# Expert items of 128 rows with an fp32 tail of up to 32 rows, in place of items of one or two 128-row blocks

## The reference

```python
logits = (xt @ w_router + b_router)
top_val, top_idx = lax.top_k(logits, TOP_K)      # 4 of 32 experts for each of 1024 tokens
gates = jax.nn.softmax(top_val, axis=-1)
...
gu = rows @ w_gate_up[e] + b_gate_up[e]          # 1024 -> 2048
gate = jnp.minimum(gu[:, :D_FF], SWIGLU_LIMIT)
up = jnp.clip(gu[:, D_FF:], -SWIGLU_LIMIT, SWIGLU_LIMIT)
hid = (up + 1.0) * (gate * jax.nn.sigmoid(gate * SWIGLU_ALPHA))
return hid @ w_down[e] + b_down[e]               # 1024 -> 1024
```

## Time and profile before

| | |
|---|---|
| median of 3 executions | 2768.33 us (2766.95 to 2768.82) |
| the profiled execution | 2765.02 us |
| its span in the profile | 2763.4 us |
| granted TensorE clock, mean | 0.965 of full speed |
| busy: PE, DVE, ACT | 92%, 62%, 48% |
| expert stage, first bias row on PE to last store of `ysb` | 844.4 to 2547.3 us of the span |

### The profile page before, as it was taken

One profiled execution on the slowest core, in us unless ns is written; L12 is line 12 of the kernel. 1 busy time (PEld: TensorE's weight loads), 2 busy tenths in 40 slices (PEclk: granted clock), 3 DMA queues, 4 the chain that ended last, 5 costly groups with the idle time before them and its releaser, 6 DMA issues.

```text
span 2763.4 us, 37051 instructions
## 1 busy us (share of the span) xinstructions
PE 2537.6 (92%) x11003; PEld 1855.1 (67%) x11004; DVE 1701.2 (62%) x2447; ACT 1318.7 (48%) x1535; POOL 201.5 (7%) x188
## 2 busy tenths in 40 slices
PE   6999999868848999999999999999999999998687
PEld 3456666544426778787777878787878888777233
DVE  4653333523355796779779696768676657774354
ACT  2113333332223774658577484657564445562232
POOL 1100000001220000000000000000000000000210
PEclk9999999988868999999999999999999999999799
DMA  5009500322215896879789696869685666783541
GB/s 177 19 12 339 186 20 22 109 81 69 68 42 187 301 355 215 293 242 369 240 302 354 217 348 237 290 226 341 218 286 199 203 207 231 246 286 129 192 144 49
DMA packets 387538, 556.36 MB, mean 201 GB/s; under 512 B 18241, under 2 KB 326977, under 8 KB 387362
## 3 DMA queue, kind: packets, MB, share of 16 engines
q1 hardware_dynamic: 333922, 456.55, 49.4%
q10 hardware_dynamic: 39408, 57.67, 5.7%
q0 software_dynamic: 14160, 41.51, 4.4%
HBM read 482.91 MB, written 71.19 MB: 201 GB/s over the span
## 4 chain that ended last, share of the span: by engine, by line
PE 63%; issue 6%; DVE 6%; ACT 1%; DMA 1%; DVEq 1%; SPq 0%; ACTq 0%; POOLq 0%; POOL 0%
PE bank L554 16%; PE bank L552 16%; PE bank L553 16%; PE bank L1274 5%; PE bank L647 4%; PE bank L546 2%; PE bank L523 1%; DVE wlo L711 1%; PE bank L531 1%; PE bank L650 1%; DVE sig L732 1%; PE bank L1286 1%; DVE xlo L716 1%; DVE gat L727 0%; DVE upc L728 0%
## 5 line engine op out<-in xcount | busy, mean ns | idle before, releaser
L1458 ACT ACTIVATE whi<-raw 128x2048 fp32r<-128x2048 f32 x384 | 733.4, 1917 | 578.5 <-PE bank L554 532.2
L711 DVE TENSOR_TENSOR wlo<-raw,whi 128x2048 fp32r<-128x2048 f32 x384 | 876.2, 2286 | 210.4 <-PE bank L554 195.6
L552 PE MATMUL bank<-whi,xhi 128*128 128x512 f32 x1472 | 577.1, 392 | 0.0
L554 PE MATMUL bank<-wlo,xhi 128*128 128x512 f32 x1472 | 574.3, 390 | 0.0
L553 PE MATMUL bank<-whi,xlo 128*128 128x512 f32 x1472 | 573.8, 390 | 0.0
L554 PEld LDWEIGHTS bank<-wlo,xhi 128*128 128x128 f32 x1472 | 276.5, 188 | 58.1
L553 PEld LDWEIGHTS bank<-whi,xlo 128*128 128x128 f32 x1472 | 276.8, 188 | 57.1
L552 PEld LDWEIGHTS bank<-whi,xhi 128*128 128x128 f32 x1472 | 276.9, 188 | 54.1
L552 PE MATMUL bank<-whi,hhi 128*128 128x512 f32 x736 | 292.1, 397 | 0.0
L554 PE MATMUL bank<-wlo,hhi 128*128 128x512 f32 x736 | 287.3, 390 | 0.0
L553 PE MATMUL bank<-whi,hlo 128*128 128x512 f32 x736 | 287.0, 390 | 0.0
(11 more groups left out here) (263 smaller groups left out, 2853.6 us busy)
## 6 DMA issues: line engine op xcount, KB each, us to landing
raw<-in_w_gate_up_dram SPq DMA_DIRECT2D x512, 512.0 KB, 4.7
raw<-in_w_down_dram SPq DMA_DIRECT2D x128, 1024.0 KB, 6.9
expert_rows<-zeros ACTq DMA_DIRECT2D x1, 32768.0 KB, 103.8
expert_rows<-ysb ACTq DMA_DIRECT2D x46, 512.0 KB, 6.2
xall<-in_x_dram SPq DMA_DIRECT2D x8, 512.0 KB, 10.2
uT<-in_w_out_dram SPq DMA_DIRECT2D x1, 4096.0 KB, 14.2
xr<-in_x_dram SPq DMA_DIRECT2D x8, 512.0 KB, 6.4
h_scratch<-h SPq DMA_DIRECT2D x8, 512.0 KB, 2.8
```

Source lines behind the costliest of these rows:

```text
L552: pe.matmul(dst, stat_hi[:, b, kt], hi, start=False, stop=False)
L554: return pe.matmul(dst, stat_hi[:, b, kt], lo, start=False, stop=last)
L711: dve.tensor_tensor(wlo[:, c % LO], raw[:, c % RAW], whi[:, c % HI].bitcast(F32), ALU.subtract).then_inc(lo_ready, 1)
L1458: act.activation(whi[:, c % HI], raw[:, c % RAW], ACT.Copy).then_inc(hi_ready, 1)
```

## The change

- The item table: an item is one expert with up to 128 rows. Rows 129 to 160 of an expert are a *tail* of its item (the field `TWO` now means "has a tail"). An expert with more than 160 rows gets a further item, which loads and splits all its weights again. There are no two-block items. With the counts above this makes 38 items, of which 8 have a tail: 32 experts, and a second item for 6 of them.
- A tail's rows are multiplied in plain fp32 with the raw pieces in `raw`, not with whi and wlo. `tail_piece` puts four products with 32 stationary columns on four column groups of the array. For gate/up each group takes one of the four 128-deep parts of the piece, and `tail_sum` adds the four groups with one product by a 0/1 matrix. For down each group makes 256 of the 1024 columns. ACT, DVE and PE do sigmoid, clamp, product and transposes for the tail with their own small buffers (`tail_sigmoid`, `tail_gated`, `turn_tail_hidden`, `tail_hidden`).
- SP may overwrite a slot only when PE's tail product has read it too (`tail_free`, in `slot_free`).
- POOL fetches the tail's rows and the expert's biases, spread to 32 partitions.
- The transposes of the next item's rows are cut into two halves, after pieces 7 and 9.
- The second group of the item loop now runs: 6 of its 32 passes have an item, 26 have none.

The core of the difference:

```diff
-BLK = 2 * P
-MAX_ITEMS = E + T * TOPK // (BLK + 1)
+TAIL = 32
+GROUPS = P // TAIL
+MAX_ITEMS = E + T * TOPK // (P + TAIL + 1)
...
+                                    body(n, k1, True)
                                     eng.reg_add(self.twos, self.twos, 1)
                                 with eng.Else():
-                                    body(n, k1, (0,))
-
-        def gate_bank(blocks, b, q):
-            return banks(2 * b + q % 2) if len(blocks) == 2 else banks(2 + q % 2)
-
-        def down_bank(b, d):
-            return banks(2 * b + d)
+                                    body(n, k1, False)
...
+            def turn_tail_rows(n, k1):
+                pe.wait_ge(xgt_in, 16 * k1 + 16)
+                hold(pe, xlo_ready, 2 * n + 2)
+                for k in range(KD):
+                    mm = pe.transpose(banks(XT)[:, k * TAIL:k * TAIL + TAIL], xgt[0:TAIL, k * P:k * P + P],
+                                      ident[0:TAIL, 0:TAIL])
+                mm.then_inc(xtt_done, 1)
...
+            def tail_piece(k1, c):
+                if c == 0:
+                    pe.wait_ge(xt_ready, k1 + 1)
+                    pe.wait_ge(ytail_ready, k1)
+                if c in (2, 4, 6, 8):
+                    pe.wait_ge(sums_ready, 4 * k1 + c // 2)
+                if c >= 8:
+                    pe.wait_ge(ht_ready, 4 * k1 + c - 7)
+                if c < 8:
+                    half = c % 2
+                    for j in range(GROUPS):
+                        mm = pe.matmul(banks(ACC)[j * TAIL:j * TAIL + TAIL, :], xt[:, half * 4 + j], raw[:, c % RAW, j],
+                                       start=(half == 0), stop=(half == 1))
+                else:
+                    r = c - 8
+                    for kk in range(2):
+                        for j in range(GROUPS):
+                            mm = pe.matmul(banks(ACC)[j * TAIL:j * TAIL + TAIL, 0:256], htail[:, 2 * r + kk],
+                                           raw[:, c % RAW, 2 * kk + j // 2, j % 2 * 256:j % 2 * 256 + 256],
+                                           start=(r == 0 and kk == 0), stop=(r == 3 and kk == 1))
+                mm.then_inc(tail_free, 1)
+            def tail_sum(k1, j):
+                pe.wait_ge(sums_ready, 4 * k1 + j + 1)
+                pe.wait_ge(ht_ready, 4 * k1 + j)
+                pe.matmul(banks(SUM)[0:TAIL, :], sel[:], sums[:], start=True, stop=True).then_inc(u_done, 1)
+            def turn_tail_hidden(k1, j):
+                hold(pe, hid_t_ready, 4 * k1 + j + 1)
+                for h in range(2):
+                    mm = pe.transpose(banks(SUM)[:, h * TAIL:h * TAIL + TAIL], hid_t[0:TAIL, h * P:h * P + P],
+                                      ident[0:TAIL, 0:TAIL])
+                mm.then_inc(htt_done, 1)
...
+                    mm = gate_piece(n, c) if c < 8 else down_piece(n, c)
+                    mm.then_inc(w_free, 1)
+                    if c in (3, 5, 7):
+                        turn_hidden(n, (c - 3) // 2)
+                    if tail:
+                        if c in (2, 4, 6, 8):
+                            tail_sum(k1, c // 2 - 1)
+                        if c in (3, 5, 7, 9):
+                            turn_tail_hidden(k1, (c - 3) // 2)
+                        tail_piece(k1, c)
                     if c == 4:
                         items.ahead(n + 1)
                         nxt, nxt2 = items.value(LIVE), items.value(TWO)
+                    if c in (7, 9):
+                        with pe.If(nxt > 0):
+                            turn_rows(n + 1, (c - 7) // 2)
+                    if c == 11:
                         with pe.If(nxt2 > 0):
+                            turn_tail_rows(n + 1, nk1)
...
+            def tail_sums(k1, j):
+                if j == 0:
+                    dve.wait_ge(bias_t_in, 80 * k1 + 80)
+                dve.wait_ge(u_done, 4 * k1 + j)
+                dve.wait_ge(tail_free, PIECES * k1 + 2 * j + 2)
+                dve.tensor_tensor(sums[:].rearrange("p (h n) -> p h n", h=2),
+                                  banks(ACC).rearrange("p (h n) -> p h n", h=2),
+                                  bias_t[:].rearrange("p (h q n) -> p h q n", h=2, q=4)[:, :, j, :],
+                                  ALU.add).then_inc(sums_ready, 1)
+            def tail_clamp(k1, j):
+                src = banks(SUM)[0:TAIL]
+                dve.wait_ge(u_done, 4 * k1 + j + 1)
+                dve.wait_ge(hid_t_ready, 4 * k1 + j)
+                dve.tensor_scalar(gat_t[0:TAIL], src[:, 0:256], LIMIT, None, ALU.min).then_inc(gat_t_ready, 1)
+                dve.tensor_scalar(upc_t[0:TAIL], src[:, 256:512], LIMIT, -LIMIT, ALU.min, ALU.max).then_inc(upc_t_ready, 1)
+            def tail_gated(k1, j):
+                dve.wait_ge(sig_t_done, 4 * k1 + j + 1)
+                dve.tensor_tensor(sig_t[0:TAIL], gat_t[0:TAIL], sig_t[0:TAIL], ALU.mult).then_inc(gs_t_done, 1)
+                dve.wait_ge(gs_t_done, 4 * k1 + j + 1)
+                dve.wait_ge(htt_done, 4 * k1 + j)
+                dve.scalar_tensor_tensor(out=hid_t[0:TAIL], in0=upc_t[0:TAIL], scalar=1.0, in1=sig_t[0:TAIL],
+                                         op0=ALU.add, op1=ALU.mult).then_inc(hid_t_ready, 1)
+            def tail_rows(k1):
+                dve.wait_ge(tail_free, PIECES * k1 + PIECES)
+                dve.wait_ge(ytail_out, 64 * k1)
+                dve.tensor_tensor(ysb_t[:], banks(ACC)[:, 0:256], bias_d[:], ALU.add).then_inc(ytail_ready, 1)
...
+                    if tail and c in (3, 5, 7, 9):
+                        tail_gated(k1, (c - 3) // 2)
                     if c in (1, 3, 5, 7):
+                        dve.wait_ge(w_free, PIECES * n + c + 1)
+                        clamp(n, (c - 1) // 2)
+                        if tail:
+                            tail_sums(k1, (c - 1) // 2)
...
+                            two, tails = read(sp, n, TWO), read(sp, n, NTWO)
+                            def slot_free(c):
+                                read_by_tail = sp.snap(tails * PIECES + two * (c + 1), min_val=0, max_val=MAX_ITEMS * PIECES)
+                                hold(sp, lo_ready, PIECES * n + c + 1)
+                                sp.wait_ge(tail_free, read_by_tail)
                             for c in range(RAW, PIECES):
-
-                                sp.wait_ge(lo_ready, PIECES * n + c - RAW + 1)
+                                slot_free(c - RAW)
                                 expert_piece(sp, e, c, c % RAW)
                                 if c == RAW:
                                     sp.reg_mov(live_r, read(sp, n + 1, LIVE))
@@ -986,14 +1082,17 @@
                                 sp.reg_mov(expert_r, read(sp, n + 1, EXPERT))
                                 e2 = sp.snap(expert_r, min_val=0, max_val=E - 1)
                                 for c in range(RAW):
-                                    sp.wait_ge(lo_ready, PIECES * n + RAW + c + 1)
+                                    slot_free(RAW + c)
...
+                    k = read(pool, n, NTWO)
+                    e = read(pool, n, EXPERT)
+                    hold(pool, xtt_done, k)
+                    pool.dma_start(ids_t[0:TAIL], list_dram[bass.ds(row + P, TAIL), :]).then_inc(ids_t_in, 16)
+                    hold(pool, ids_t_in, 16 * k + 16)
+                    pool.indirect_dma_start(out=xgt[0:TAIL], out_offset=None, in_=u2_dram,
+                                            in_offset=bass.IndirectOffsetOnAxis(ap=ids_t[0:TAIL], axis=0)
+                                            ).then_inc(xgt_in, 16)
+                    hold(pool, ytail_ready, k)
+                    pool.dma_start(bias_t[0:TAIL], b_gate_up[0, bass.ds(e, 1), :].rearrange("e n -> (e n)")
+                                   .partition_broadcast(TAIL)).then_inc(bias_t_in, 16)
...
+            def tail_sigmoid(k1, j):
+                act.wait_ge(gat_t_ready, 4 * k1 + j + 1)
+                act.activation(sig_t[0:TAIL], gat_t[0:TAIL], ACT.Sigmoid, scale=ALPHA).then_inc(sig_t_done, 1)
+            def tail_hidden(k1, j):
+                act.wait_ge(htt_done, 4 * k1 + j + 1)
+                act.activation(htail[:, 2 * j:2 * j + 2].rearrange("p k n -> p (k n)"), banks(SUM)[:, 0:2 * TAIL],
+                               ACT.Copy).then_inc(ht_ready, 1)
...
+            def tail_rows_out(k1, row):
+                act.wait_ge(ytail_ready, k1 + 1)
+                for j in range(GROUPS):
+                    act.dma_start(y_dram[bass.ds(row + P, TAIL), j * 256:j * 256 + 256],
+                                  ysb_t[j * TAIL:j * TAIL + TAIL]).then_inc(ytail_out, 16)
...
+                        sigmoid(n, (c - 1) // 2)
+                    if tail and c in (2, 4, 6, 8):
+                        tail_sigmoid(k1, c // 2 - 1)
                     if c in (3, 5, 7):
+                        hidden(n, (c - 3) // 2)
+                    if tail and c in (3, 5, 7, 9):
+                        tail_hidden(k1, (c - 3) // 2)
...
```

(9 more changed lines are left out.)

425 lines of the change are left out of this document (208 added, 217 removed).

## The result

| | before | changed |
|---|---|---|
| median of the runs | 2768.32 us | 3103.24 us (3101.77 to 3105.25, 4 runs) |
| ratio to before | | 1.1216, 95% interval 1.1200 to 1.1233 |
| profiled execution, its span | 2765.02, 2763.4 | 3103.04, 3101.4 |
| mean granted clock | 0.965 | 0.915 |
| expert stage, first bias row to last store | 1702.9 | 842.6 to 2866.7, 2024.1 |

The change makes the kernel 12% slower. The prediction was 3000 us, slower, with a range of 2895 to 3120. The sign and the range hold; the number is 103 us low.

A forecast was written before the change was run, and what follows sets the result against it. It took the expert stage to be bound by PE, busy 92% of the span. 2765.0 + 211 (expert stage) + 17 (empty passes) + 4 (start) = 2997, with 3.3 for the median 3000 us, range 2895 to 3120.

The forecast's parts named there:

- The ring: Items with a tail: slot release, load, ACT's split and next tail product wait in turn; eight whole loads, 72.4 us.
- rival 1: The ring does not bind and an item with a tail is DVE-bound at about 50 us: 2640 us in all; chance 5%.
- Eight links: Steps 2 to 9 and 9 to 11 of an item with a tail, each holding a whole load; sum 72.4 us.
- T: An item with a tail: 97 us, against 70.4 for the two-block item it replaces.
- Pieces 0 to 2 before the ring: Start of an item with a tail: 3 x 3 us and a sum, 10.1 us.
- The last T: The last item with a tail loads no next item, so links 6 to 9 run at PE's pace: 80 us.
- S after a T: One-block item after a tail item: raw slots empty, late splits, 1.5 us for each of 6, 9 in all.
- S: A one-block item without a tail: unchanged except for halved transposes, 38.1 us each, 30 of them 1143 us.
- A rival with the right number and the wrong cause: Runs of one-block items are held by DMA, 39 us or more each: 3030 us in all; chance 8%.
- Column groups: A tail piece's four products on four column groups overlap: 0.85 us a piece, bounds 0.43 and, with no overlap, 3.4.
- Changes of the tile's shape: 24 changes of shape on PE in an item with a tail, left unpriced; at 0.15 us each, 29 us more in all.
- Empties: At the expert stage's end each engine passes 26 empty items at 0.65 us: +17 us, bounds 8 and 74.

The follow-up runs named there:

- the order mended: Against the second form: in one-block items too ACT's split stands last in its step, ACT's and DVE's next-item columns come first in steps 8 and 10; 2695.2 us.
- the second form: Changed kernel with GROUP 19, DVE's columns first in step 9, and in tail items each ACT split a whole step later; 2753.2 us, ratio 0.9949.
- The shorter load: Changed kernel with half of piece 11 not loaded, so half of that piece's products use old weights; 3090.7 us, ratio 1.118.

## Why the prediction was right, and where it was 103 us short

**The ring (its rival 1, refuted) was right, in mechanism and in size.** Eight links were priced at 72.4, with tail pieces and clock at 84.4. In the tail item from 1187.3 SP issues the load that tail piece 2 releases (down piece 8), and the one that tail piece 11 releases (the first half of the next item's gate piece 5), at these times:

```profile
1203.28 32.03 SPq L484 DMA_DIRECT2D raw<-in_w_down_dram  x4
...
1288.24 0.37 SPq L477 DMA_DIRECT2D raw<-in_w_gate_up_dram  x1
```

That is 85.0 us. The two runs that cut into the ring, at ACT or at SP, took most of T's excess away. Inside it one term was not priced, ACT's table load of 1.28 us ahead of the first sigmoid. ScalarE: Activation LUTs ("What ACT_TABLE_LOAD costs") of the Trainium skill has the same 1283 ns, but adds a drain that makes it 2.66 us; here the load starts as the split ends, and the sigmoid starts 0.02 us after the load, so this case does not show the drain. One sign was named too low: PE was to be half busy in the ring.

```profile
1187.30:1192.00 4.70, 4.15 (x17) 3.25 (x16) 1.82 (x1) 2.18 (x2) 0.00 (x0) 0.69 0.75 223
...
1204.00:1288.00 84.00, 53.53 (x243) 30.95 (x241) 35.31 (x47) 22.45 (x27) 2.32 (x2) 0.82 0.33 110
```

It is busy 53.5 us of the 84.0, or 64%, at a mean granted clock of 0.82.

**T: 97 predicted, 105.7 measured.** The two ends of the ring were mis-sized.
- "Pieces 0 to 2 before the ring take 3 x 3 us and a sum", 12.7 with their tail pieces. It took 16.0, from 1187.3 to 1203.3. The prediction took the full clock there; in the first 4.7 us the mean granted clock is 0.69 (the first line above). That this is all of the 3.3 us is not shown.
- The prediction let T end with the ring. But after tail piece 11 has released its slot it is 4.7 us to the store, because ACT copies the rows only after it has split a piece whose load was issued at 1284.3.

Seven T together: +61. The last T was predicted at 80 and took 77.6.

**S after a T: +1.5 predicted, about +7 measured**, 33 us over six. The step "the raw slots are empty and the next S starts with late splits" saw the late pieces but not who stands behind them. ACT in the S that starts at 1292.9, in order of time:

```profile
1298.93 1.28 ACT L1572 ACT_TABLE_LOAD   x1 [1.52 <-PE bank L586]
1300.32 1.91 ACT L1572 ACTIVATE whi<-raw 128x2048 fp32r<-128x2048 f32 x1
1303.59 1.91 ACT L1572 ACTIVATE whi<-raw 128x2048 fp32r<-128x2048 f32 x1 [1.36 <-DMA raw<-in_w_gate_up_dram]
1305.52 1.28 ACT L1586 ACT_TABLE_LOAD   x1
1306.81 0.42 ACT L1586 ACTIVATE sig<-gat 128x256 f32<-128x256 f32 x1
```

DVE had the gate ready at 1297.5. ACT takes its sigmoid at 1306.8, behind the splits of pieces 6 and 7, of which the second waits for its load, and behind two table loads. DVE idles 7.2 us for it and PE 7.0 us for DVE. It is the same order that makes the ring. Late loads and the order both have a part: with the loads out of the ring and ACT's order as it was such an S took 42.0, and with the order mended 4.4 less than in the second form.

**S: 38.1 predicted, 38.98 measured**, 22 us over 24. "An S stays as it is: its transposes are halved, nothing else" is the failed step. The second half of transposes needs the bank that the first half leaves, so a chain PE, ACT, DVE, PE now runs inside pieces 8 and 9, and PE waits 1.2 us at its end. PE's wait ahead of these transposes in the S from 955.1 of the kernel before, and its other wait in the S from 1337.7 now:

```profile
PE bank L523 <- issue: 0.2, 1, 0.2
```
```profile
PE bank L573 <- DVE hlo L803: 0.6, 1, 0.6
```

All of PE's named waits come to 1.0 us in the first of these items and to 1.8 in the second, which is nearly all of the loss of 0.9 us. That it is order and not PE's work or the loads is shown: with the halves kept and ACT's splits last in their steps, S takes 36.5 us early in a row and PE waits 0.4 of them. A rival with the right number and the wrong cause stood close by: 39 us by DMA. The shorter load refuted it.

**Column groups:** four at once, and 0.85 us for a piece at the full clock was right, but by luck. The prediction took a record for a product. Each product is two records, 0.43 us apart at the full clock and 0.86 at half. The 16 records of the full-width line of the earlier trace rows are the eight products of one sum over k in the source, so a full-width fp32 product takes 0.86 us too (7.03 / 8 is 0.88), and the lower bound of 0.43 could not be reached. The eight records on 64 rows are four products, two at a time, and their stretch (570.8 to 574.2) has a granted clock of 0.61, not 1.00. So an fp32 product costs the same on a part of the array as on all of it; what column groups give is four of them in the time of one. The prediction set the Trainium skill's four passes for true FP32 (FP8 and Floating Point Precision, "TensorE Precision Notes") against the full width; by the estimate of 0.85 us made from them there, the trace agrees at full width too.

**Changes of the tile's shape:** set aside in the prediction, at 29 us if each cost 0.15. Runs show that they do cost something. A down piece of the last T, at the full clock:

```profile
2861.50 0.39 PE L586 MATMUL bank<-wlo,hhi 128*128 128x512 f32 x1
2861.82 1.07 PE L639 MATMUL bank<-raw,htail 128*32 128x256 f32 x16
2862.82 0.50 PE L584 MATMUL bank<-whi,hhi 128*128 128x512 f32 x1
2863.16 0.40 PE L585 MATMUL bank<-whi,hlo 128*128 128x512 f32 x1
```

Products of one shape follow each other here at 0.23 us, and the 16 records of 256 columns, four at a time, need 4 x 0.215. From the first line to the last that would be 1.32 us, and it is 1.66. So a tail piece costs about 0.3 us more than its products, 4 us in a T of 12 pieces and some 30 in eight, as an estimate. Where a load sets the pace this is partly hidden; where PE does, it is part of T's 56 to 58 us.

**Empties: 17 predicted.** Last store to the end grew by 18.6 us, and the chain shows a pass each 0.66 us. Right, and branches are not dear: no empty pass took longer. The Trainium skill's rule on a taken branch (Runtime: NRT & Kernel Launch, "Instruction fetch mechanics") is for a target outside the pages of instructions that an engine holds; no stall of that kind shows, and no run tells whether these jumps leave those pages.

**Start: +4 predicted, -1.8 measured.** Neither can be told: in the other profiled executions, whose start is the same but for a step or two of the table, the first bias row comes at 841.1 to 845.6 us.

The sum: T +61 - 2.4 - 3 (for biases, not seen), S after T +33, S +22, that is +110 in the stage; end +1.6; start -5.8: 106 over the predicted span of 2995. The profiled execution is this time at the median and not 3.3 below it, and 103 are left.

## What to carry to other kernels

When a buffer gets a second and later reader, follow its release through every engine's queue: if the release waits for something that stands behind the next load's consumer, each step costs a whole load, however idle the engines are. On an engine that both takes in loads and serves a short chain, put the chain's work ahead of the wait for a load, and give the load a step of slack; here this, with the same order for the next item's columns and 0.4% from fewer empty passes, turned 12% slower into 2.6% faster. Then read the item after the odd one too: it starts with what the odd one left unloaded.

## What was not expected of the hardware

- Four fp32 products with 32 stationary columns each, on four column groups and into one bank, take as long as one of them: 1.94 us against 1.92 at the low clock, 1.06 for the four at the full one.
- A change between that shape and full-width products costs PE about 0.3 us for each tail piece, both ways together; the profile counts it as busy.
- Small idle times cost twice. In T with the ring the mean granted clock is 0.84, and PE's busy time 73.3 us; with nearly the same products and 3.1 us of idle time it is 1.00 and 55.3. Of the 47 us between them 18 are PE's own work at the lower level.
- ACT loads a table of 1.28 us twice in each item, ahead of the split of step 0 and ahead of the item's first sigmoid. In the mended order, one of the two is gone in each of the eight tail items (30 in place of 38 loads on the split's line).
